# First loads and pooled products of the merge stage moved into the last rows of the attention stage

## The chip, the cores and the metric

The kernel runs on one core of a Trainium2 chip. The metric is the time of one launch on the device, in microseconds, lower is better. Five engines with a queue each share the work: PE (TensorE, matrix products), DVE (VectorE), ACT (ScalarE), POOL (GpSimd) and SP (SyncE, which here only issues DMAs). They wait for each other and for DMAs through semaphores.

## The reference

One layer of a hybrid backbone over 2048 latent tokens and 256 context tokens, width 1024, everything in float32. The normalised input is projected once, and its columns feed four mixers of width 256: a gated MLP over chunks (`gm`), a neighbourhood attention (`na`), a recurrence (`rw`) and centred pooling (`pl`). The end, with which this case deals, is:

```
pl = pool_mix(pl_p) * silu(pl_g)      # (centred mean - p) @ w_grp, times a scale per channel
na = natten_latent(q, k, v, ...) * silu(na_g)   # 32 rows of 64 tokens, 8 x 16 window + 256 context keys

gates = sigmoid(merge_logits)                           # (2048, 4 * 1024)
y = gates[:, 0:1024] * (gm @ w_br[0])
for i in 1..3:
    y = y + gates[:, i*1024:(i+1)*1024] * (branch_i @ w_br[i])   # branches gm, na, rw, pl
out = rmsnorm(x + gate * (y @ w_out), final_g)
```

## The kernel before

Three stages follow each other: `front_stage` (the projections), `recurrence_stage`, and `late_stages`, which calls `attention_stage` (L2053 and on) and `merge_and_output_stage` (L2385). Each stage is a block of five instruction streams, one for each engine, written out by hand; at the end of a block stands a barrier of all engines (it bears the line L2046 in the trace). No scheduler moves anything: the order on an engine is the order of the text, and only semaphores tie the engines.

**Attention.** A loop over 32 rows of the grid runs as a pipeline of depth four: in step n, PE computes the scores of row n, the values of row n-2 (L2353), turns the probabilities of row n-1 (L2335, L2339) and turns the output of row n-2 (L2366). DVE adds the bias and takes the maximum (L2257), copies, divides (L2283) and multiplies by the gate (L2270, one step later). ACT takes the exponentials. Steps 32 to 34 drain the pipeline. Side jobs ride along: POOL computes the pooled differences, DVE scales the eight row blocks of `w_out` by the residual gate (L2294, steps 23 to 30). After the last step come, one after the other, the pooled branch's eight products (PE L2375, four blocks of two) and DVE's scaling and gating of them (L2302, in place in `pg`, which lives in the tile `v_t`). ACT has by then taken SiLU of the pooled gate in one instruction (L2248). SP stores the attention's output in three parts (rows 0-15, 16-27, 28-31; L2144) and the pooled output in four blocks (L2148) to `branchT` in DRAM, waits until all have landed (L2149, L2150), and only then joins the barrier.

**Merge.** The 2048 tokens are handled in four blocks of 512 (n), each in 16 units (branch i = 0..3, pair p = 0..3 of output tiles of 128 columns). Products are made in three passes of split operands: for an operand a, ACT writes `a_hi` (a rounded copy) and DVE `a_lo = a - a_hi` over a's own place; PE adds hi*hi, lo*hi and hi*lo. A unit is 12 matmuls of 512 columns (L2647 to L2649). DVE multiplies each by its gate tile (L2568) and, from the second branch on, adds it to y (L2574). In the first block only, DVE also makes the low parts of the branch weights (L2550, eight halves; `mw`), of the branch rows (L2554; `mb`), of y (L2562) and of `w_out` (L2558). Then y @ w_out follows (tile_upper, tile_lower, tile: L2661 to L2692), the residual and the final norm. At the start SP issues, in this order: the first half of branch 0's weights (L2447), branch 0's rows (L2437), gate tiles 0 and 1 (L2433), the second half (L2451), gate tiles 2 and 3, the whole weights of branch 1 (L2445), branch 1's rows. Weights of branches 2 and 3 are loaded whole, one after pair 1 of each of the first two branches. A unit (0, i, 0) with i > 0 waits for both weight halves of its branch.

Of the kernel before, what the change touches and what calls it, by code (L numbers as in the profile page):

```python
# [2038 lines left out]
def attention_stage(nc, t, s):  # L2039
# [6 lines left out]
    with ExitStack() as ctx:  # L2046
# [24 lines left out]
        pl_ps, pl_out, pl_silu, pl_stored = sem("pool_products"), sem("pool_out_ready"), sem("pool_silu"), sem("pool_stored")  # L2071
# [10 lines left out]
        stored, gate_out, gate_in, scaled = sem("na_stored"), sem("gate_row_out"), sem("gate_rows_in"), sem("wo_scaled")  # L2082
# [21 lines left out]
        def _(sp):  # L2104
# [27 lines left out]
            for first, end in PARTS:  # L2132
                if first == PARTS[1][0]:
# [15 lines left out]
            sp.wait_ge(stored, 64 * len(PARTS))  # L2149
            sp.wait_ge(pl_stored, 16 * NB)  # L2150
# [61 lines left out]
        def _(act):  # L2212
# [35 lines left out]
            A.activation(pg, pg, ACT.Silu).then_inc(pl_silu, 1)  # L2248

        @block.vector  # L2250
        def _(dve):
# [44 lines left out]
            dve.wait_ge(pl_silu, 1)  # L2296
            for b in range(NB):
                dve.wait_ge(pl_ps, b + 1)
# [7 lines left out]
        def _(pe):  # L2306
# [49 lines left out]

            for n in STEPS:
# [10 lines left out]
            pe.wait_ge(diff_set, 2)  # L2368
            pe.wait_ge(plw_in, 16 * 5)
            bvg.after(pe, ROWS - 1, "g")  # L2370
            for b in range(NB):
                if b >= 2:
                    pe.wait_ge(pl_out, b - 1)
                for p in range(2):
                    last = T.matmul(ps[:, 2 * (b % 2) + p, :], plw[:, p, :], dd[:, p, b * BLK:(b + 1) * BLK], start=True, stop=True)  # L2375
                last.then_inc(pl_ps, 1)

def merge_and_output_stage(nc, t, s):
# [8 lines left out]
    with ExitStack() as ctx:  # L2388
# [3 lines left out]
        def split(name, shape):  # L2392
# [4 lines left out]
            return rows, sb(f"{name}_hi", shape, F32R), lo  # L2397
        wo, wo_lo = s["wo_rows"][:, 0:KT * D].rearrange("p (k n) -> p k n", k=KT), s["wo_lo"]
        wo_hi = sb("wo_hi", [P, KT, D], F32R)
        w, w_hi, w_lo = split("mw", [P, 4, 2, D])  # L2400
        y, y_hi, y_lo = split("y", [P, KT, BLK])
        br, b_hi, b_lo = split("mb", [P, 2, 2, BLK])
        gate = sb("m_gate", [P, 4, 2, BLK])
# [3 lines left out]
        w_in, w_h, w_l = [sem(f"w_in{i}") for i in range(5)], sem("w_hi_ready"), sem("w_lo_ready")  # L2407
        b_in, b_h, b_l = [sem("b_in0"), sem("b_in1")], sem("b_hi_ready"), sem("b_lo_ready")
        wo_h, wo_l = sem("wo_hi_ready"), sem("wo_lo_ready")
        gate_in = [[sem(f"gate_in{p}{par}") for par in range(2)] for p in range(NP)]  # L2410
# [12 lines left out]
        w_brs = t["w_br"].rearrange("l i (k p) n -> p (l i) k n", p=P)  # L2423
        plain = lambda a: a.bitcast(F32)
        pair = lambda a, p: a[:, 2 * p:2 * p + 2, :]

        w_part = lambda a, i, h: a[:, 0, :, h * BLK:(h + 1) * BLK] if i == 0 else a[:, i, h, :]

        @block.sync
        def _(sp):  # L2430
            def load_gate(n, i, p):
                src = t["gatesT"][8 * i + 2 * p:8 * i + 2 * p + 2, :, n * BLK:(n + 1) * BLK]
                sp.dma_start(gate[:, p, :, :], src.rearrange("m p t -> p m t")).then_inc(gate_in[p][i % 2], 16)  # L2433

            def load_b(n, i):
                src = t["branchT"][2 * i:2 * i + 2, :, n * BLK:(n + 1) * BLK]
                sp.dma_start(br[:, i % 2, :, :], src.rearrange("m p t -> p m t")).then_inc(b_in[i % 2], 16)  # L2437

# [5 lines left out]
            def load_w(i):  # L2444
                sp.dma_start(w[:, i, :, :], w_brs[:, i, :, :]).then_inc(w_in[i], 16)  # L2445
# [319 lines left out]
```

## Time and profile before

| | us |
|---|---|
| median of 3 runs | 2583.83 (2577.88 to 2587.68) |
| profiled execution | 2572.3 |
| its span, first to last instruction | 2570.6 |
| PE busy | 2270.5 (88%) |
| DVE busy | 1560.4 (61%) |
| ACT busy | 1015.1 (39%) |
| first product of the merge starts at | 2192.36 |
| first product of y @ w_out as a full tile (L2690) | 2271.9 |

### The profile page before, as it was taken

To read this page: it belongs to the slowest core of one execution; us is meant where nothing else is said; L and a number is where in the kernel's file an instruction comes from. 1 tells how busy PE (TensorE), PEld (TensorE's weight loads), DVE (VectorE), ACT (ScalarE), POOL (GpSimd) and SP (SyncE) were. 2 spreads that over 40 slices of the span, in tenths; PEclk is the share of its full clock that TensorE was granted. 3 is DMA by queue.
4 is the path that set the end of the run, shared out by engine and by line. 5 is a ranking of instruction groups with operands and counts; after the bars stand their busy time and mean duration, and the time that the engine had idled before them with its cause. 6 is when DMAs were issued, how large, how long until landed. Compare 5 with 4: busy or idle time off the path is not lost. (4 is left out here: it accounts for less than half of the span.)

```text
span 2570.6 us, 65138 instructions
## 1 busy us (share of the span) xinstructions
PE 2270.5 (88%) x26434; PEld 1854.1 (72%) x26434; DVE 1560.4 (61%) x2583; ACT 1015.1 (39%) x1739; POOL 188.5 (7%) x260
## 2 busy tenths in 40 slices
PE   4999999999899999999668787778695797799998
PEld 2788878888688878888556676667565575677787
DVE  5756656667755456666366666666363577756744
ACT  5454234444522124444345444545323665311111
POOL 0000000000000000000120010000032650000000
PEclk7999999999999999999879999999797899899999
DMA  6343333332333233333321111110356521734542
GB/s 229 110 135 115 108 113 99 112 115 98 119 99 106 88 102 108 110 118 103 92 57 35 34 43 34 35 34 20 115 191 201 134 92 51 278 123 164 197 140 89
DMA packets 253116, 279.50 MB, mean 109 GB/s; under 512 B 34411, under 2 KB 177899, under 8 KB 250347
## 3 DMA queue, kind: packets, MB, share of 16 engines
q1 hardware_dynamic: 250602, 267.94, 32.7%
q10 hardware_dynamic: 2304, 8.39, 0.8%
q8 instruction: 178, 2.92, 0.5%
q14 instruction: 32, 0.25, 0.0%
HBM read 184.66 MB, written 91.62 MB: 107 GB/s over the span
## 5 line engine op out<-in xcount | busy, mean ns | idle before, releaser
L715 PE MATMUL proj_ps<-h_hi,w_hi 128*128 128x512 f32 x1656 | 650.0, 393 | 28.8 <-DVE h_lo L465 20.8
L716 PE MATMUL proj_ps<-h_lo,w_hi 128*128 128x512 f32 x1656 | 646.9, 391 | 0.0
L717 PE MATMUL proj_ps<-h_hi,w_lo 128*128 128x512 f32 x1656 | 646.6, 390 | 0.0
L318 ACT CAST w_hi<-w_raw 128x512 fp32r<-128x512 f32 x420 | 255.1, 621 | 695.8 <-PE proj_ps L717 353.1
L715 PEld LDWEIGHTS proj_ps<-h_hi,w_hi 128*128 128x128 f32 x1656 | 312.5, 189 | 99.1 <-issue 27.7
L717 PEld LDWEIGHTS proj_ps<-h_hi,w_lo 128*128 128x128 f32 x1656 | 312.2, 189 | 65.7
L716 PEld LDWEIGHTS proj_ps<-h_lo,w_hi 128*128 128x128 f32 x1656 | 312.7, 189 | 63.5
L482 DVE TENSOR_TENSOR w_lo<-w_raw,w_hi 128x512 fp32r<-128x512 f32 x420 | 283.1, 688 | 44.2 <-ACT w_hi L318 43.8
L498 DVE TENSOR_TENSOR z_slots<-proj_ps,x_rows 128x512 f32<-128x512 f32 x174 | 120.2, 691 | 171.1 <-PE proj_ps L717 169.0
L498 DVE TENSOR_TENSOR x_rows<-proj_ps,x_rows 128x512 f32<-128x512 f32 x116 | 80.2, 691 | 109.7 <-PE proj_ps L717 103.7
L2647 PE MATMUL late_ps<-mb_hi,mw_hi 128*128 128x512 f32 x256 | 102.5, 400 | 26.3 <-DVE mb_lo L2554 19.3
L1140 DVE TENSOR_TENSOR inv_g<-rw_ps,level_masks 128x512 f32<-128x512 f32 x90 | 62.0, 689 | 95.7 <-PE rw_ps L1308 95.5
L2648 PE MATMUL late_ps<-mb_lo,mw_hi 128*128 128x512 f32 x256 | 101.4, 396 | 0.0
L2649 PE MATMUL late_ps<-mb_hi,mw_lo 128*128 128x512 f32 x256 | 101.3, 396 | 0.0
L1256 ACT COPY inv<-rw_ps 128x512 f32<-128x512 f32 x72 | 42.2, 587 | 148.7 <-PE rw_ps L1308 148.6
L2257 DVE CUSTOM_DVE_ANT_0 scores<-na_ps,bias_windows 128x768 f32<-128x768 f32 x64 | 61.2, 956 | 61.0 <-PE na_ps L2328 40.0
L980 POOL MEMSET rpb_padded<- 60x127 f32 x1 | 0.2, 197 | 1264.2 <-POOLq L89 1264.2
L494 DVE COPY x_rows<-proj_ps 128x512 f32<-128x512 f32 x58 | 40.1, 691 | 73.6 <-PE proj_ps L717 73.6
L2228 ACT ACTIVATE probs<-scores,softmax_stats 128x768 f32<-128x768 f32 x64 | 60.1, 940 | 53.7 <-DVE softmax_stats L2260 53.7
L2690 PE MATMUL late_ps<-wo_hi,y_hi 128*128 128x512 f32 x208 | 81.3, 391 | 0.0
L2691 PE MATMUL late_ps<-wo_lo,y_hi 128*128 128x512 f32 x208 | 80.9, 389 | 0.0
L2692 PE MATMUL late_ps<-wo_hi,y_lo 128*128 128x512 f32 x208 | 80.9, 389 | 0.0
(343 smaller groups left out, 3934.1 us busy)
## 6 DMA issues: line engine op xcount, KB each, us to landing
w_raw<-in_w_in SPq DMA_DIRECT2D x240, 256.0 KB, 3.0
scratch_gatesT<-z_slots SPq DMA_DIRECT2D x128, 256.0 KB, 2.7
m_gate<-scratch_gatesT SPq DMA_DIRECT2D x64, 512.0 KB, 3.9
scratch_zT<-z_slots SPq DMA_DIRECT2D x108, 256.0 KB, 2.4
ada<-in_ada_w SPq DMA_DIRECT2D x4, 2048.0 KB, 15.2
mb_rows<-scratch_branchT SPq DMA_DIRECT2D x16, 512.0 KB, 4.8
x_res<-in_x SPq DMA_DIRECT2D x16, 512.0 KB, 4.6
out<-x_res ACTq DMA_DIRECT2D x16, 512.0 KB, 2.6
```

What stands on the lines that cost most here:

```text
L318: A.copy(wh[:, i, :, :], raw[:, q, :, :]).then_inc(w_hi, 1)
L482: V.tensor_tensor(wl[:, i, :, :], raw[:, W_SOURCE[i], :, :], wh[:, i, :, :].bitcast(F32), ALU.subtract).then_inc(w_lo, 1)
L498: V.tensor_tensor(to, ps[:, BANK[n], :], part[:, {1: 0, 3: 0, 4: 2, 5: 0, 6: 1}[n], :], ALU.add).then_inc(ev, 1)
L715: T.matmul(out, wh[:, i, k, :], hi[:, o, k, :], start=(first and k == 0), stop=False, skip_group_check=not first)
L716: T.matmul(out, wh[:, i, k, :], lo[:, o, k, :], start=False, stop=False, skip_group_check=not first)
L717: last = T.matmul(out, wl[:, i, k, :], hi[:, o, k, :], start=False, stop=(k == 3), skip_group_check=not first)
L2647: T.matmul(o, hi, b_hi[:, i % 2, k, :], start=(k == 0), stop=False)
L2648: T.matmul(o, hi, b_lo[:, i % 2, k, :], start=False, stop=False)
L2649: last = T.matmul(o, lo, b_hi[:, i % 2, k, :], start=False, stop=(k == 1))
L2690: T.matmul(o, y_hi[:, k, rows], wo_hi[:, k, cols], start=(k == 0), stop=False)
L2691: T.matmul(o, y_hi[:, k, rows], wo_lo[:, k, cols], start=False, stop=False)
L2692: last = T.matmul(o, y_lo[:, k, rows], wo_hi[:, k, cols], start=False, stop=(k == KT - 1))
```

## The change

In words: (1) the semaphores and the places of the merge's raw tiles (`merge_gate`, `merge_rows`, `merge_w`) are set up ahead of the attention; they lie over the attention's `q_t`, `k_t` and further on. As soon as the last row's scores are done (q and k are read no more) and `w_out` has been scaled, SP issues branch 0's two weight halves, its rows and its four gate tiles. (2) Pooled blocks 0 and 1 are multiplied by PE inside steps 32 and 33 of the attention, ahead of the turn of the output; blocks 2 and 3 stay behind the last step. ACT's SiLU of the pooled gate is cut into four. (3) SP no longer waits for the landing of the stores ahead of the barrier, but behind it, ahead of the loads of branch 1; DVE waits for the attention's stores before its first multiply. (4) All branch weights are now loaded in column halves, and a unit of pairs 0 or 2 waits only for the half that it reads. (5) In the first block, DVE's low parts stand in another place: weight halves behind pairs 1 and 3 (branch 0) or 0 and 2 (branches 1, 2), the rows' low part behind pair 2 (branch 0) or pair 1; ACT's order follows. The rest only moves tiles.

```diff
@@ attention, SP
             for first, end in PARTS:
...
+                if end == ROWS:
+                    fp.after(sp, ROWS - 1, "S")
+                    sp.wait_ge(scaled, KT)
+                    load_merge_w(sp, t, s, 0, 0)
+                    load_merge_rows(sp, t, s, 0, 0)
+                    load_merge_gate(sp, t, s, 0, 0, 0)
+                    load_merge_gate(sp, t, s, 0, 0, 1)
+                    load_merge_w(sp, t, s, 0, 1)
+                    load_merge_gate(sp, t, s, 0, 0, 2)
+                    load_merge_gate(sp, t, s, 0, 0, 3)
                 bvg.after(sp, end - 1, "g")
...
-            sp.wait_ge(stored, 64 * len(PARTS))
-            sp.wait_ge(pl_stored, 16 * NB)
@@ attention, ACT and DVE
-            A.activation(pg, pg, ACT.Silu).then_inc(pl_silu, 1)
+            for b in range(NB):
+                c = slice(b * BLK, (b + 1) * BLK)
+                A.activation(pg[:, :, c], pg[:, :, c], ACT.Silu).then_inc(pl_silu, 1)
...
-            dve.wait_ge(pl_silu, 1)
             for b in range(NB):
+                dve.wait_ge(pl_silu, b + 1)
@@ attention, PE
+            def pool_products(b):
+                if b == 0:
+                    pe.wait_ge(diff_set, 2)
+                    pe.wait_ge(plw_in, 16 * 5)
+                    fv.after(pe, ROWS - 1, "b1")
+                if b >= 2:
+                    pe.wait_ge(pl_out, b - 1)
+                for p in range(2):
+                    last = T.matmul(ps[:, 2 * (b % 2) + p, :], plw[:, p, :], dd[:, p, b * BLK:(b + 1) * BLK], start=True, stop=True)
+                last.then_inc(pl_ps, 1)
...
                     turn_probs(n - 1)
+                if n >= ROWS and n < ROWS + 2:
+                    pool_products(n - ROWS)
                 if valid(n - 2):
                     bvr.after(pe, n - 2, "o")
...
+            pool_products(2)
+            pool_products(3)
@@ merge, SP
+            sp.wait_ge(s["na_stored"], 64 * 3)
+            sp.wait_ge(s["pl_stored"], 16 * NB)
+            load_merge_w(sp, t, s, 1, 0)
+            load_merge_rows(sp, t, s, 0, 1)
+            load_merge_w(sp, t, s, 1, 1)
...
-                        if n == 0 and i < 2 and p == 1:
-                            load_w(i + 2)
+                        if n == 0 and i < 2 and p in (1, 2):
+                            load_merge_w(sp, t, s, i + 2, p - 1)
@@ merge, ACT (likewise for branches 2 and 3)
             split_w(1, 0)
+            split_b(0, 1)
             split_w(1, 1)
-            split_b(0, 1)
@@ merge, DVE
             split_w(0, 1)
+            dve.wait_ge(s["na_stored"], 64 * 3)
...
-                        if n == 0 and i < 3 and p < 2:
-                            split_w(i + 1, p)
-                        if p == 2 and (i < 3 if n == 0 else i in (1, 2)):
+                        if n == 0 and i < 3 and p in ((0, 2) if i else (1, 3)):
+                            split_w(i + 1, 0 if p < 2 else 1)
+                        if p == (1 if i else 2) and (i < 3 if n == 0 else i in (1, 2)):
                             split_b(n, i + 1)
@@ merge, PE
-                if n == 0 and (i == 0 and p % 2 == 0 or p == 0):
-                    pe.wait_ge(w_l, 2 * i + 2 if i else p // 2 + 1)
+                if n == 0 and p % 2 == 0:
+                    pe.wait_ge(w_l, 2 * i + p // 2 + 1)
@@ new
+def load_merge_w(sp, t, s, i, h):
+    src = t["w_br"].rearrange("l i (k p) n -> p (l i) k n", p=P)[:, i, :, h * BLK:(h + 1) * BLK]
+    sp.dma_start(s["merge_w"][:, i, :, h * BLK:(h + 1) * BLK], src).then_inc(s["w_in"][i][h], 16)
```

How the order changes at three places. The first is the end of PE's attention, before: the values (`v_even`), turned probabilities (`probs`) and outputs (`o_rows`) of rows 30 and 31, then the pooled products (`pool_diff`).

```order
L2353 MATMUL na_ps<-v_even,probs_t 64x64 x24
L2335 MATMUL na_ps<-ident,probs 128x128 x8
L2339 MATMUL na_ps<-ident,probs 128x128 x4
L2366 MATMUL na_ps<-ident,o_rows 128x128
L2353 MATMUL na_ps<-v_even,probs_t 64x64 x24
L2366 MATMUL na_ps<-ident,o_rows 128x128
L2375 MATMUL na_ps<-pool_diff,v_t 128x512 x8
```

The same place on PE in the changed kernel.

```order
L2364 MATMUL na_ps<-v_even,probs_t 64x64 x24
L2346 MATMUL na_ps<-ident,probs 128x128 x8
L2350 MATMUL na_ps<-ident,probs 128x128 x4
L2376 MATMUL na_ps<-pool_diff,v_t 128x512 x2
L2391 MATMUL na_ps<-ident,o_rows 128x128
L2364 MATMUL na_ps<-v_even,probs_t 64x64 x24
L2376 MATMUL na_ps<-pool_diff,v_t 128x512 x2
L2391 MATMUL na_ps<-ident,o_rows 128x128
L2376 MATMUL na_ps<-pool_diff,v_t 128x512 x4
```

Two of the four pooled blocks now stand ahead of the turns of rows 30 and 31. The second place is SP around the end of the attention stage, before: the pooled output's stores, the end of the block, and the merge's first loads.

```order
L2148 DMA scratch_branchT<-v_t 128x2x512 x4
L2046 UNCONDITIONAL_BRANCH
L2429 UNCONDITIONAL_BRANCH
L2447 DMA mw_rows<-in_w_br 128x2x512
L2437 DMA mb_rows<-scratch_branchT 128x2x512
L2433 DMA m_gate<-scratch_gatesT 128x2x512 x2
L2451 DMA mw_rows<-in_w_br 128x2x512
L2433 DMA m_gate<-scratch_gatesT 128x2x512 x2
L2445 DMA mw_rows<-in_w_br 128x2x1024
L2437 DMA mb_rows<-scratch_branchT 128x2x512
```

SP in the changed kernel, from the second row of branch 0's early loads to the loads of branch 1.

```order
L2742 DMA mb_rows<-scratch_branchT 128x2x512
L2737 DMA m_gate<-scratch_gatesT 128x2x512 x2
L2747 DMA mw_rows<-in_w_br 128x2x512
L2737 DMA m_gate<-scratch_gatesT 128x2x512 x2
L2155 DMA scratch_branchT<-na_gate 64x256 x4
L2159 DMA scratch_branchT<-v_t 128x2x512 x4
L2046 UNCONDITIONAL_BRANCH
L2446 UNCONDITIONAL_BRANCH
L2747 DMA mw_rows<-in_w_br 128x2x512
L2742 DMA mb_rows<-scratch_branchT 128x2x512
L2747 DMA mw_rows<-in_w_br 128x2x512
```

Seven loads now stand ahead of the last stores of the attention; behind the block's end only branch 1's three are left. The third place is DVE in branch 0 of the merge, before: low parts of weights (`mw_lo`) and rows (`mb_lo`) between the multiplies (`y_rows<-m_gate,late_ps`).

```order
L2550 TENSOR_TENSOR mw_lo<-mw_rows,mw_hi 128x2x512
L2568 TENSOR_TENSOR y_rows<-m_gate,late_ps 128x1024
L2550 TENSOR_TENSOR mw_lo<-mw_rows,mw_hi 128x1024
L2568 TENSOR_TENSOR y_rows<-m_gate,late_ps 128x1024
L2550 TENSOR_TENSOR mw_lo<-mw_rows,mw_hi 128x1024
L2568 TENSOR_TENSOR y_rows<-m_gate,late_ps 128x1024
L2554 TENSOR_TENSOR mb_lo<-mb_rows,mb_hi 128x1024
L2568 TENSOR_TENSOR y_rows<-m_gate,late_ps 128x1024
```

The same stretch of DVE in the changed kernel.

```order
L2552 TENSOR_TENSOR mw_lo<-mw_rows,mw_hi 128x2x512
L2570 TENSOR_TENSOR y_rows<-m_gate,late_ps 128x1024 x2
L2552 TENSOR_TENSOR mw_lo<-mw_rows,mw_hi 128x2x512
L2570 TENSOR_TENSOR y_rows<-m_gate,late_ps 128x1024
L2556 TENSOR_TENSOR mb_lo<-mb_rows,mb_hi 128x1024
L2570 TENSOR_TENSOR y_rows<-m_gate,late_ps 128x1024
L2552 TENSOR_TENSOR mw_lo<-mw_rows,mw_hi 128x2x512
```

The second weight half of branch 1 now stands behind all four multiplies, and the rows' low part ahead of the last one.

## Rows read from the trace of the kernel before

**Rows 1.** Chain of waits from 2160 to 2195: start us, us, what.
```profile
2184.03 0.37 SPq L2447
...
2184.45 5.44 DMA mb_rows<-scratch_branchT
...
2189.91 1.05 ACT mb_hi L2486
...
2190.99 1.24 DVE mb_lo L2554
...
2192.36 0.76 PE late_ps L2647
2193.13 0.43 PE late_ps L2648
```
**Rows 2.** Timeline, PE and DVE, end of attention: start us, us, engine line, [idle before <-releaser].
```profile
2168.01 0.27 PE L2366 MATMUL na_ps<-ident,o_rows 128*128 128x128 f32 x1
2168.21 0.69 DVE L2287 COPY probs_t<-na_ps 128x512 f32<-128x512 f32 x1 [1.10 <-PE na_ps L2339]
...
2169.24 1.62 PE L2353 MATMUL na_ps<-v_even,probs_t 128*64 128x64 f32 x48 [0.96 <-DVE na_gate L2270]
...
2171.68 0.29 DVE L2270 TENSOR_TENSOR na_gate<-na_ps,na_gate 128x128 f32<-128x128 f32 x1 [0.42 <-PE na_ps L2366]
...
2172.12 7.25 PE L2375 MATMUL na_ps<-pool_diff,v_t 128*128 128x512 f32 x16 [0.48 <-DVE na_gate L2270]
...
2174.21 1.41 DVE L2302 SCALAR_TENSOR_TENSOR v_t<-na_ps,pool_scale,v_t 128x512 f32<-128x512 f32 x2 [2.24 <-PE na_ps L2375]
...
2179.41 1.41 DVE L2302 SCALAR_TENSOR_TENSOR v_t<-na_ps,pool_scale,v_t 128x512 f32<-128x512 f32 x2 [0.31 <-PE na_ps L2375]
2180.85 0.36 SPq L2148 DMA_DIRECT2D scratch_branchT<-v_t  x1
```
**Rows 3.** Timeline, PE alone, starts of branches 1 to 3, first block.
```profile
2207.84 0.47 PE L2647 MATMUL late_ps<-mb_hi,mw_hi 128*128 128x512 f32 x1 [1.56 <-issue]
...
2221.69 0.47 PE L2647 MATMUL late_ps<-mb_hi,mw_hi 128*128 128x512 f32 x1 [2.71 <-issue]
...
2237.14 0.47 PE L2647 MATMUL late_ps<-mb_hi,mw_hi 128*128 128x512 f32 x1 [2.70 <-issue]
```
**Rows 4.** Timeline, DVE alone, the merge's first block.
```profile
2210.93 1.22 DVE L2568 TENSOR_TENSOR m_gate<-m_gate,late_ps 128x1024 f32<-128x1024 f32 x1 [2.06 <-PE late_ps L2649]
2212.18 1.22 DVE L2574 TENSOR_TENSOR y_rows<-y_rows,m_gate 128x1024 f32<-128x1024 f32 x1
2213.33 1.22 DVE L2550 TENSOR_TENSOR mw_lo<-mw_rows,mw_hi 128x1024 fp32r<-128x1024 f32 x1
...
2226.37 1.22 DVE L2568 TENSOR_TENSOR m_gate<-m_gate,late_ps 128x1024 f32<-128x1024 f32 x1 [2.39 <-PE late_ps L2649]
...
2240.23 1.22 DVE L2568 TENSOR_TENSOR m_gate<-m_gate,late_ps 128x1024 f32<-128x1024 f32 x1 [0.80 <-PE late_ps L2649]
...
2254.74 9.16 DVE L2558 TENSOR_TENSOR wo_lo<-wo_rows,wo_hi 128x1024 fp32r<-128x1024 f32 x8
```
**Rows 5.** Chain of waits from 1900 to 2400: the last piece of tile_lower in block 0.
```profile
2264.85 7.25 PE late_ps L2668 x32
```
**Rows 6.** Windows by stage: last column GB/s, ahead of it DMA share and PEclk.
```profile
2208.00:2222.00 14.00, 11.29 (x50) 9.03 (x49) 11.83 (x11) 6.87 (x7) 0.00 (x0) 1.00 0.84 306
2222.00:2237.00 15.00, 12.45 (x48) 9.78 (x46) 12.47 (x12) 3.05 (x3) 0.00 (x0) 0.89 0.67 235
```
**Rows 7.** Windows of 1 us around the clock's fall and rise (PEclk after the busy times).
```profile
2183.00:2184.00 1.00, 0.00 (x0) 0.00 (x0) 0.00 (x0) 0.00 (x0) 0.00 (x0) 1.00 0.10 35
2184.00:2185.00 1.00, 0.00 (x0) 0.00 (x0) 0.00 (x0) 0.00 (x0) 0.00 (x0) 0.78 0.00 0
...
2198.00:2199.00 1.00, 1.00 (x5) 0.82 (x4) 1.00 (x1) 0.00 (x0) 0.00 (x0) 0.89 1.02 397
```
**Rows 8.** SP's own waits from 2150 to 2260.
```profile
SPq L2150 <- DMA scratch_branchT<-v_t: 2.4, 1, 2.4
```
**Rows 9.** Timeline, DVE alone, last two scalings of w_out, one in each attention row.
```profile
2154.10 1.21 DVE L2294 TENSOR_TENSOR wo_rows<-wo_rows,q_t 128x1024 f32<-128x1024 f32 x1
...
2159.38 1.22 DVE L2294 TENSOR_TENSOR wo_rows<-wo_rows,q_t 128x1024 f32<-128x1024 f32 x1
```
**Rows 10.** Issue to landing from 2150 to 2260: count, KB each, median us.
```profile
m_gate<-scratch_gatesT SPq DMA_DIRECT2D x20, 512.0 KB, 4.6
```

More of the change, by code:

```diff
@@ L2366, in _ @@
                     bot.done(T.transpose(ps[:, 7, BR:BR + P], on[:], s["ident"][:]), "OT")
[L2368 to L2376, printed above, removed]
+            pool_products(2)
+            pool_products(3)
 def merge_and_output_stage(nc, t, s):
@@ L2406, in merge_and_output_stage @@
         ps = ctx.enter_context(nc.psum_tensor("late_ps", [P, 4, 2, BLK], F32))
[L2407 to L2408 removed]
+        w_in, w_h, w_l = s["w_in"], sem("w_hi_ready"), sem("w_lo_ready")
+        b_in, b_h, b_l = s["rows_in"], sem("b_hi_ready"), sem("b_lo_ready")
         wo_h, wo_l = sem("wo_hi_ready"), sem("wo_lo_ready")
[L2410 removed]
+        gate_in = s["gate_in"]
         units, gated, added = sem("merge_products"), sem("gated"), sem("y_added")
@@ L2511, in _ @@
             split_w(3, 0)
+            split_b(0, 3)
             split_w(3, 1)
-            split_b(0, 3)
             for n in range(NB):
@@ L2714, in late_stages, with load_merge_gate, load_merge_rows @@
         s["wo_lo"] = ctx.enter_context(nc.sbuf_tensor("wo_lo", [P, KT, D], F32R))
-        with ExitStack() as edges:
-            edges.enter_context(nc.sbuf_tensor("wo_rows_end", [P, 8 * EDGE], F32))
-            s["wo_in"] = ctx.enter_context(nc.semaphore("wo_in"))
-            attention_stage(nc, t, s)
-        merge_and_output_stage(nc, t, s)
+        ctx.enter_context(nc.sbuf_tensor("wo_rows_end", [P, 8 * EDGE], F32))
+        with ExitStack() as under:
+            s["merge_gate"] = under.enter_context(nc.sbuf_tensor("m_gate", [P, 4, 2, BLK], F32))
+            s["merge_rows"] = under.enter_context(nc.sbuf_tensor("mb_rows", [P, 2, 2, BLK], F32))
+            s["merge_w"] = under.enter_context(nc.sbuf_tensor("mw_rows", [P, 4, 2, D], F32))
+        s["wo_in"] = sem("wo_in")
+        s["gate_in"] = [[sem(f"gate_in{p}{par}") for par in range(2)] for p in range(4)]
+        s["rows_in"] = [sem("b_in0"), sem("b_in1")]
+        s["w_in"] = [[sem(f"w_in{i}{h}") for h in range(2)] for i in range(4)]
+        s["na_stored"], s["pl_stored"] = sem("na_stored"), sem("pool_stored")
+        attention_stage(nc, t, s)
+        merge_and_output_stage(nc, t, s)
+def load_merge_gate(sp, t, s, n, i, p):
+    src = t["gatesT"][8 * i + 2 * p:8 * i + 2 * p + 2, :, n * BLK:(n + 1) * BLK]
+    sp.dma_start(s["merge_gate"][:, p, :, :], src.rearrange("m p t -> p m t")).then_inc(s["gate_in"][p][i % 2], 16)
+def load_merge_rows(sp, t, s, n, i):
+    src = t["branchT"][2 * i:2 * i + 2, :, n * BLK:(n + 1) * BLK]
+    sp.dma_start(s["merge_rows"][:, i % 2, :, :], src.rearrange("m p t -> p m t")).then_inc(s["rows_in"][i % 2], 16)
+def load_merge_w(sp, t, s, i, h):
+    src = t["w_br"].rearrange("l i (k p) n -> p (l i) k n", p=P)[:, i, :, h * BLK:(h + 1) * BLK]
+    sp.dma_start(s["merge_w"][:, i, :, h * BLK:(h + 1) * BLK], src).then_inc(s["w_in"][i][h], 16)
 STAGES = (front_stage, recurrence_stage, late_stages)
```

42 lines of the change are left out of this document (13 added, 29 removed).

## The prediction

> **What bounds the kernel now.** I read the page first: PE is busy for 88% of the span and the chain that ended last runs along PE's merge products, so time is won only where PE waits. Then the chain of waits at the hand-over [rows 1]: the merge's first product starts at 2192.36 and hangs, backwards, on DVE's low part of the rows (1.24), ACT's cast (1.05), a DMA of 5.44 and an issue at 2184.03. The timeline shows PE's last attention work, the pooled products, from 2172.12 for 7.25, to 2179.4 [rows 2]. PE thus stands still for 13.0 us, and all of the merge's input travels in that hole. Third, the merge's first block: PE waits again at the starts of branches 1, 2 and 3, 1.56, 2.71 and 2.70 [rows 3]. DVE is the pace there: a multiply starts 1.25 before its add, the next operation 1.15 later [rows 4]. A branch is four multiplies, four adds and three low parts: 4 x (1.25 + 1.14) + 3 x 1.14 = 13.0 us on DVE, against 4 units x 12 matmuls x 0.227 = 10.9 on PE (32 matmuls took 7.25 [rows 5]). The windows show 306 GB/s in such a branch at a DMA share of 0.84 [rows 6], so the DMAs are near full but not over. Last, the clock: it fell to 0.50 in the slice 2184 to 2185, some 5 us after PE stopped, and rose at about 2198.2 [rows 7], 5.8 us after PE began again; meanwhile a matmul took 0.43 instead of 0.227 [rows 1].
>
> **The change, part by part.** The sum is made against the profiled execution (span 2570.6, time 2572.3); the three runs lie higher, median 2583.83, so I carry the difference over to that median.
>
> *End of the attention.* PE's turn of row 31's probabilities ends at 2168.0; the pooled block 0 now comes next, four instructions of 0.43 = 1.7. The turn of row 30's output goes from 2168.01 to 2169.75, its gating ends at 2170.4 (DVE's copy of 2168.21 to 2168.90 is no longer in its way) and the values of row 31 start at 2170.5, not 2169.24 [rows 2]. They take 1.62, block 1 another 1.7, so row 31 is gated at 2174.15 to 2174.45, 2.5 later than the 2171.68 of before. DVE's pooled scaling follows at once: 2174.45, where it was 2174.21. Block 2 may start on PE when block 0 has been read, 2175.9; its result is there 2.05 later (2172.12 to 2174.21 was 2.09 [rows 2]), DVE has it done at 2179.4, block 3 at 2181.1. Before it was 2180.8. The products moved up gain nothing: +0.25. Cutting SiLU in four costs ACT some 0.3 in all and hides, as DVE needs the first quarter only at 2174.45.
>
> *The hand-over.* Before, SP issued its last store at 2180.85 (0.36), waited 2.4 for the landing [rows 8], to 2183.6, and issued the merge's first load at 2184.03; so barrier and branch took 0.4. Now SP arrives at 2181.1 + 0.4 and all engines pass at 2181.95. Branch 0's data are there: SP may issue them when the last scores and the last scaling of w_out are done, 2159.38 + 1.22 = 2160.6 [rows 9]; seven loads of 512 KB are 3.67 MB, 12 us at the 306 GB/s of [rows 6], plus the 4.6 of one load [rows 10]: by 2177 at the latest. Behind the barrier the splits stay on the path, which DMA no longer covers: ACT's cast 1.05, then DVE's two low parts, 1.14 and 1.24, 0.14 to PE: 2181.95 + 1.1 + 1.14 + 1.24 + 0.14 = 2185.5. Before 2192.36: 6.8 earlier.
>
> *Branch 1's loads* are issued when the last pooled store has landed, 2183.9. Three of 512 KB at the 4.6 to landing of [rows 10] and 1.4 more for each next are down by 2191.2. DVE wants the first at 2195.3 (below), so this hides with 4 us to spare.
>
> *Branch 0's products.* PE now stands still for 6 us (2179.65 to 2185.5), longer than the 5 after which the clock fell, so I take it to fall just as PE starts and to come back 5.7 after, at 2191.2, as before. That costs the same 2.8 in both kernels: no gain. Units end at 2190.6, 2193.7, 2196.5, 2199.2. DVE follows: multiplies at 2191.0, 2194.1, low part of the weight half 2195.3, multiply 2196.9, rows 2198.0, multiply 2199.6, second half 2200.7. The rows' low part ends at 2199.2 just as PE is through, so the wait of 1.56 at branch 1 goes.
>
> *Branches 1 to 3.* DVE's first multiply of branch 1 starts at 2202.4, where it was 2210.93 [rows 4]: 8.5 earlier. From here DVE never waits: three stretches of 13.0, to 2241.4, and the last low part of y to 2242.6. Before it lost 2.39, 0.80 and some 0.5 to PE [rows 4] and was through at 2254.74 - the gain has grown to 12.1. On PE the branch 2 wait of 2.71 goes, since its rows' low part stands two operations earlier (done 2209.6, PE needs it at 2210.2); with it goes the half clock that followed, in the slices of 2222 to 2237 at 0.89 [rows 6], 1.6 us of PE. Of the 2.70 at branch 3 1.5 stays, and in the first tile, which waits for y's four low parts, PE waits some 2 more than before. All this is inside DVE's sum.
>
> *Tail of the block.* Last low part of y to the end of tile_lower: before 2254.74 to 2264.85 + 7.25 = 2272.1, 17.4 [rows 4, 5]; now 17.1. So the block ends at 2259.7, 12.4 earlier. Blocks 1 to 3 are untouched and shift whole.
>
> The DMA pieces of 2 KB instead of 4 KB in the weights of branches 1 to 3 I cost at nothing: the gate tiles, of the same 2 KB pieces, make most of those 306 GB/s. If that fails, the second weight halves are late by at most one landing, 4.6, of which 4 is covered. The 3.67 MB that now land in SBUF while rows 28 to 31 are worked: no row shows such a load beside that loop; I bound it from zero to 1.5 us (a tenth of the 14 us it lies beside, at 5.28 a row [rows 9]) and take zero, as multiplies of 128x1024 took the same 1.22 at 306 GB/s [rows 4, 6].
>
> Sum: 0.25 lost, in all 12.4 gained; 2572.3 - 12.4 = 2559.9, and on the median 2583.8 - 12.4 = 2571.4.
>
> **The rivals.**
>
> *The clock stays up.* In the old kernel it fell 5 us into the hole; the new hole is 6. If it falls later or comes back a step earlier, branch 0 runs at 2.4 GHz, up to 2.8 of PE. Worked through DVE's chain the block ends at 2256.9 to 2258: gain 14 to 15, time 2569. Against it: 6 is more than 5.
>
> *A slow start behind the barrier.* In the old trace ACT, DVE and PE had 4.6 us between the barrier's release at 2184.0 and ACT's first cast, which waited for data; anything they did in it was hidden. Now it would show. For it: no row shows these engines starting at once there. Against: SP's first issue came 0.4 after its landing, branch included. Price from 0 to 4.6 at the start; since DVE's chain then wastes less on PE, 8 to 10 of gain is left: time 2574. The Trainium skill, Runtime: NRT & Kernel Launch, section Instruction fetch mechanics, says that a taken branch whose target lies outside the fetched pages stalls until a DMA has brought them. By that rule the change would be in this rival; the trace neither shows nor excludes it.
>
> *The gain is given back inside the merge.* The early part needs loads of branches 1 and 2 closer together. If they land late, the chain is held by DMA at about the old distances and only part of the 6.8 stays: gain 4 to 5, time 2579. Against it: the slack of 4 us above, and 0.84 of DMA share. That the early loads don't become early (SP held behind the stores of part 2) belongs here; those were issued at 2155, so I hold it for unlikely.
>
> *Slower: the clock doesn't come back.* The new first block has waits of about 1.5, 1, 1.7 and 1.7 close together after branch 2. If PE's clock stays at 1.2 GHz through the 16 units, they take 16 x 12 x 0.43 = 82 instead of 46: the block ends at 2290, 18 later than before, time 2601. It decides where more than some 35 us of the block run at half clock (to 2222: about equal). For it: a wait of 2.71 was followed by half clock [rows 3, 6]. Against it: the old kernel, with more waits, lost only one such piece. The Trainium skill, TensorE: Matmul & The Clock Gate, section HAM oscillation, warns that gaps between bursts of products keep throwing the clock back. By it this rival would be likelier than the trace makes it; the granted clock of 0.89 and 1.00 in [rows 6] speaks for a single dip.
>
> **How the numbers follow.** Forecast (10.5 to 14 gained) 0.60; clock stays up 0.15; slow start 0.12; given back 0.09; slower 0.04. Less than 0.5% (12.9 us) either way is about what a measurement of this kernel can't tell from no change, and the forecast's 12.4 lies just at that edge: a good two fifths of its chance and all of the second case fall beyond it, 0.25 + 0.15 plus 0.03 for a slow start on a lucky median. Faster 0.44, within 0.5% 0.50, slower 0.06. The three runs differ by 10 us, so a median of the new kernel moves by some 4 of itself: the range goes from 2562 (clock up, low median) to 2582 (given back, high median).
>
> **What would show it.** Right: branch 0's seven loads issued about 2161; ACT's first cast within 0.2 of 2182; PE's first merge product at 2185.5; the pooled branch done at 2181, not earlier; no wait at branches 1 and 2 and one of 1.5 at branch 3; DVE without a wait from branch 1 on; tile_lower ending near 2260. Wrong: a first cast later than 2183 (slow start), half clock beyond 2195, casts of branch 1's weights that wait past 2195 for their DMA, or attention rows slower than 5.3 us each from 2161 on.

## The result and the profile after

The changed kernel took 2552.27 us (median of 4 runs, 2548.27 to 2556.73) against 2583.5 us (4 runs, 2577.88 to 2587.68): ratio 0.9881, 95% interval 0.9854 to 0.9908. A second comparison on another occasion gave 2552.31 (6 runs) against 2575.17 (21 runs), ratio 0.9927, 0.9906 to 0.9948 (the two medians by themselves divide to 0.9911). The forecast had 2571.4 with a range down to 2562, so both medians lie below it: right in its sign, 12 us gained where the medians differ by 31 and 23, and where the second ratio makes it 19.

The medians scatter by more than a part of this change is worth, so I split two traces of each kernel at three instants: the last start of attention scores, the first merge product, and the last matmul of tile_lower in block 0. Each instant is the start of that matmul. All that the change touches lies behind the first one.

| us | before | before, again | changed | changed, again | forecast for changed |
|---|---|---|---|---|---|
| start to last scores | 2159.9 | 2163.9 | 2164.4 | 2159.6 | as before |
| last scores to first merge product | 32.4 | 32.2 | 25.5 | 25.5 | 25.6 |
| first merge product to end of tile_lower | 79.4 | 79.6 | 72.7 | 73.6 | 73.8 |
| blocks 1 to 3 and the end | 298.9 | 298.9 | 290.7 | 290.7 | 298.9 |
| last scores to end | 410.7 | 410.7 | 388.9 | 389.8 | 398.3 |

The two stages that the forecast worked through agree within 1.1 us. From the last scores to the end the changed kernel is 8.5 to 9.4 us shorter than forecast, and 8.2 of these stand in the fourth row: in blocks 1 to 3, where I had written "untouched". The first median missed the forecast by 19.1; the other 10 or so are in no stage behind the last scores (see the experiment on the scatter).

The chain of waits of the changed kernel at the hand-over (start us, us, what):

```profile
2186.34 1.05 ACT mw_hi L2484
2187.40 0.02 issue
2187.42 1.23 DVE mw_lo L2552
2188.65 1.15 DVE mb_lo L2556
2189.79 0.14 issue
2189.93 0.77 PE late_ps L2650
```

Where [rows 1] had an issue and a DMA of 5.44 ahead of the cast, the chain now begins with the cast itself. The hole on PE (the time that it stands still here) went from 13.0 to 5.9. The timeline around the barrier, all engines but PE's weight loads:

```profile
2165.18 0.39 SPq L2747 DMA_DIRECT2D mw_rows<-in_w_br  x1
...
2178.86 2.72 DVE L2313 SCALAR_TENSOR_TENSOR v_t<-na_ps,pool_scale,v_t 128x512 f32<-128x512 f32 x4
2178.98 2.37 SPq L2155 DMA_DIRECT2D scratch_branchT<-na_gate  x4
2180.32 3.70 PE L2376 MATMUL na_ps<-pool_diff,v_t 128*128 128x512 f32 x8 [1.70 <-DVE v_t L2313]
2181.39 4.53 SPq L2159 DMA_DIRECT2D scratch_branchT<-v_t  x4
...
2184.13 1.41 DVE L2313 SCALAR_TENSOR_TENSOR v_t<-na_ps,pool_scale,v_t 128x512 f32<-128x512 f32 x2 [0.31 <-PE na_ps L2376]
2186.34 1.04 ACT L2484 CAST mw_hi<-mw_rows 128x1024 fp32r<-128x1024 f32 x1 [8.22 <-PEq L2046]
```

SP's last issue ends at 2181.39 + 4.53 = 2185.92 and ACT casts 0.42 later: that is the barrier, branch included. (DVE's last scaling had ended 0.38 ahead of SP's issue.) The pooled scaling ends 21.1 behind the last scores' start; in [rows 2] it was 20.9 (2180.8 - 2159.9).

PE's waits in the first block and the tiles behind it, from the timeline of PE alone, to be compared with [rows 3]:

```profile
2189.93 0.77 PE L2650 MATMUL late_ps<-mb_hi,mw_hi 128*128 128x512 f32 x1 [5.91 <-DVE mb_lo L2556]
2225.73 0.47 PE L2650 MATMUL late_ps<-mb_hi,mw_hi 128*128 128x512 f32 x1 [1.28 <-issue]
2237.56 0.47 PE L2664 MATMUL late_ps<-wo_hi,y_hi 128*128 128x512 f32 x1 [0.66 <-issue]
```

The waits at branches 1 and 2 are gone, 1.28 is left at branch 3. And the lists of PE's waits in blocks 1 to 3 (waited for, us in all, times, longest): of the kernel before, from 2270 to 2580,

```profile
PE late_ps L2647 <- DVE mb_lo L2554: 6.4, 6, 1.1
```

and of the changed kernel, from its tile_lower's end at 2263 to 2553, an empty list. Six waits, at the starts of branches 2 and 3 of blocks 1, 2 and 3. The profile's page of the kernel before had held them too, in the last number of this row, 19.3 where the hand-over accounts for 13.0:

```profile
L2647 PE MATMUL late_ps<-mb_hi,mw_hi 128*128 128x512 f32 x256 | 102.5, 400 | 26.3 <-DVE mb_lo L2554 19.3
```

One of the six on PE of the kernel before, with what DVE did there:

```profile
2316.68 0.50 PE L2647 MATMUL late_ps<-mb_hi,mw_hi 128*128 128x512 f32 x1 [1.06 <-DVE mb_lo L2554]
```

```profile
2313.01 1.22 DVE L2568 TENSOR_TENSOR m_gate<-m_gate,late_ps 128x1024 f32<-128x1024 f32 x1 [0.24 <-PE late_ps L2649]
2314.27 1.23 DVE L2574 TENSOR_TENSOR y_rows<-y_rows,m_gate 128x1024 f32<-128x1024 f32 x1
2315.41 1.22 DVE L2554 TENSOR_TENSOR mb_lo<-mb_rows,mb_hi 128x1024 fp32r<-128x1024 f32 x1
```

DVE makes the rows' low part behind pair 2's multiply and add, which themselves wait for PE's pair 2; it ends at 2316.6, while PE has been through with pair 3 since 2315.6. In the changed kernel the same three stand one pair earlier:

```profile
2301.19 1.22 DVE L2570 TENSOR_TENSOR m_gate<-m_gate,late_ps 128x1024 f32<-128x1024 f32 x1 [0.24 <-PE late_ps L2652]
2302.45 1.22 DVE L2576 TENSOR_TENSOR y_rows<-y_rows,m_gate 128x1024 f32<-128x1024 f32 x1
2303.59 1.22 DVE L2556 TENSOR_TENSOR mb_lo<-mb_rows,mb_hi 128x1024 fp32r<-128x1024 f32 x1
```

### The profile page after: what moved, and what is told of

Its sections match the earlier page's. It is cut to its first block and busy times, and to the rows that moved or that the text cites. A ratio compares the mean times of both kernels' runs of the same rounds, so it can differ in the third digit from the quotient of the medians.

```text
span 2553.3 us, 65150 instructions
## 1 busy us (share of the span) xinstructions
PE 2260.6 (89%) x26434; PEld 1847.5 (72%) x26434; DVE 1559.2 (61%) x2583; ACT 1015.4 (40%) x1742; POOL 188.6 (7%) x260
## 5 line engine op out<-in xcount | busy, mean ns | idle before, releaser
L494 DVE COPY x_rows<-proj_ps 128x512 f32<-128x512 f32 x58 | 40.0, 690 | 73.6 <-PE proj_ps L717 73.5
```

## Experiments

The kernels whose median is not given below ran once each: 2566.35 us with branch 0's loads behind the barrier, 2561.82 with the stores' landing awaited ahead of it, 2558.47 with the pooled products last, 2562.08 with the first block's old order (the kernel before: 2574.52 once, beside them), and 2550.82 with PE kept busy. One run can't tell them apart, so they are read by the stages of their traces.

**The move of the rows' low part, alone, both ways.** First the changed kernel without it in blocks 1 to 3:

```diff
-                        if p == (1 if i else 2) and (i < 3 if n == 0 else i in (1, 2)):
+                        if p == (1 if i and n == 0 else 2) and (i < 3 if n == 0 else i in (1, 2)):
                             split_b(n, i + 1)
```

> The changed kernel, but in blocks 1 to 3 DVE makes the branch rows' low part behind pair 2 again, not behind pair 1 (the first block stays as changed). Theory A (this move, which the prediction overlooked, stops a wait of 1.06 us at six branch starts, about 1.3 us each with the pipeline's refill): slower than the changed kernel by 7 to 9 us, waits of 1.06 for mb_lo back at six places, and from the last attention scores' start to the end about 397 instead of 388.9. Theory B (the extra gain of blocks 1 to 3 comes from the weights' and gates' loads or from the clock, not from this order): within 2 us of the changed kernel.

Measured: 2560.91 us (6 runs), ratio to before 0.9946 (0.9931 to 0.9960), 8.6 us above the changed kernel in the same comparison. Its trace has 397.1 from last scores to end, the stages ahead of block 1 as in the changed kernel (25.5 and 72.7), blocks 1 to 3 at 298.9, and this list of PE's waits there:

```profile
PE late_ps L2650 <- DVE mb_lo L2556: 6.4, 6, 1.1
```

Then the kernel before with that one edit:

```diff
-                        if p == 2 and (i < 3 if n == 0 else i in (1, 2)):
+                        if p == (1 if n else 2) and (i < 3 if n == 0 else i in (1, 2)):
```

> The kernel before with this one edit: in blocks 1 to 3 the rows' low part stands behind pair 1. Theory A: 7 to 9 us faster than before (ratio 0.9965 to 0.9973), the six waits gone, last scores to end about 402.5 instead of 410.7. Theory B: no change, ratio 1.000 within its interval.

Measured: 2567.73 us (10 runs), ratio 0.9967 (0.9951 to 0.9982); last scores to end 402.6, blocks 1 to 3 at 290.8, no wait there. Theory A holds in both directions, to 0.1 us in the traces; theory B falls. The move is worth 8.1 to 8.2 us by the pairs of traces, some 1.36 for each wait shown as 1.06. This trace has the loads of before and its blocks 1 to 3 take the same 290.8 as those of the changed kernel (290.7), so nothing there hangs on the weights' loads in halves.

**How large is the change, and where is the scatter.** Both kernels again, unedited.

> The changed kernel again, unedited, for a second trace and a tighter ratio. Theory A (all of the gain lies behind the last scores, 21.8 us by the two traces; the 31 us between the medians holds some 10 us of scatter): ratio nearer to 0.9915 (22 us), last scores to end 388 to 390. Theory C (the change also makes the stages ahead of the hand-over shorter, by code placement or the like): ratio stays at 0.988 and the last scores start some 10 us earlier than in the kernel before.

> The kernel before again, unedited. Shows the scatter of a ratio where nothing changed, and a second start of the last scores. Theory A: last scores to end 410 to 411 as in the first trace, while their start (2159.7 there) moves by up to 10 us. Theory C: their start lies near 2170 in most runs, against 2160 for the changed kernel.

Measured: the changed kernel 0.9927 (0.9906 to 0.9948); before against itself 0.9999 (0.9985 to 1.0014). The start of the last scores was 2159.6 (changed) and 2163.9 (before), against 2164.4 and 2159.9 in the first pair. Over all 14 traces of this study it lies between 2157.4 and 2169.1, with no tie to the kernel, since the stages ahead of it are the same in all; behind it the two traces of before agree to 0.1 us, those of the changed kernel to 0.9. Theory C falls. The gain behind the last scores is 21 to 22; the 31 us between the first medians lie outside what the stages show, and where in the runs without a trace the other 9 were was not shown.

**Branch 0's loads, behind the barrier instead of beside the attention.** The seven load calls follow the lines taken out, and stand ahead of the last line.

```diff
-                if end == ROWS:
-                    fp.after(sp, ROWS - 1, "S")
-                    sp.wait_ge(scaled, KT)
...
@@ merge, SP
...
             sp.wait_ge(s["na_stored"], 64 * 3)
```

> The changed kernel, but branch 0's seven loads are issued at the start of the merge stage, behind the barrier, not beside the last attention rows. Read by stages. Theory A (the hidden loads carry the hand-over): from the last scores to the first merge product 30 us instead of 25.5, as the first cast waits 4.6 us for its DMA; branch 1's loads queue behind them, so that first product to the end of tile_lower grows from 72.7 to some 76. Theory B (moving the stores' waits behind the barrier does it and loads of that size would land in time anyway): 25.5 to 27.

Measured: last scores to first merge product 31.8, to the end of tile_lower 73.0 more. ACT in that trace:

```profile
2196.80 1.04 ACT L2480 CAST mw_hi<-mw_rows 128x1024 fp32r<-128x1024 f32 x1 [13.99 <-DMA mw_rows<-in_w_br]
2198.47 1.04 ACT L2484 CAST mb_hi<-mb_rows 128x1024 fp32r<-128x1024 f32 x1 [0.62 <-DMA mb_rows<-scratch_branchT]
```

The first load was issued at 2191.02 and the cast came 5.8 later. Theory A's place is right, its price too low by 1.8: the first cast waited 5.8 and not 4.6, and DVE waits for the second load as well; what made the first load slower than 4.6 was not separated. So the early issue carries 6.3 of the 6.9 us of the hand-over. The expected queueing of branch 1's loads, 3 us, didn't come: 73.0 is 0.3 above 72.7, and the clock, which came back later here, explains that (below).

**The stores' landing, awaited ahead of the barrier.**

```diff
                 sp.dma_start(t["branchT"][6:8, :, c].rearrange("m p t -> p m t"), pg[:, :, c]).then_inc(pl_stored, 16)
+            sp.wait_ge(stored, 64 * len(PARTS))
+            sp.wait_ge(pl_stored, 16 * NB)
```

> The changed kernel, but SP waits for all stores to land ahead of the barrier, as before. Theory A: the barrier is 2.3 us later, last scores to first merge product 27.8 instead of 25.5, first product to wo_lo about 1 to 2 shorter or equal, since branch 1's loads start at the same instant. Theory B (barrier is held by something else): 25.5.

Measured: 28.2, then 73.1: theory A holds for the barrier, and the part expected to be equal or shorter is 0.4 longer, again by the clock (below). SP's own wait in that trace:

```profile
SPq L2161 <- DMA scratch_branchT<-v_t: 2.6, 1, 2.6
```

The same wait stands in the changed kernel too (2.6), only behind the barrier, where no engine but SP pays for it. The two terms overlap: 6.3 and 2.7 together are more than 6.9, since without early loads the casts wait for DMA in any case.

**The pooled products, all behind the last step.**

```diff
-                if n >= ROWS and n < ROWS + 2:
-                    pool_products(n - ROWS)
...
-            pool_products(2)
-            pool_products(3)
+            for b in range(NB):
+                pool_products(b)
```

> The changed kernel, but all four pooled blocks are multiplied behind the last attention step, as before. Theory A (the two early blocks delay the attention by what they save): last scores to first merge product 25.2 to 25.7 instead of 25.5, last pooled scaling within 0.3 of the changed kernel's 25.0 behind the scores' last start. Theory B (they do their work in PE's idle time and save it at the end): 27 to 29.

Measured: 24.7, then 72.8. Theory B falls, and 24.7 lies below the 25.2 to 25.7 of theory A as well: the early products do not just gain nothing, they cost 0.8 (the last pooled scaling ends 20.3 behind the last scores, not 21.1). Row 31's values wait for row 30's gating, and that for the pooled block put ahead of it. In the trace with them last, PE takes them in one piece, as it did in [rows 2], and DVE's scalings follow from 1.5 behind the gating:

```profile
2178.52 7.19 PE L2376 MATMUL na_ps<-pool_diff,v_t 128*128 128x512 f32 x16
```

```profile
2178.72 0.29 DVE L2281 TENSOR_TENSOR na_gate<-na_ps,na_gate 128x128 f32<-128x128 f32 x1 [0.42 <-PE na_ps L2389]
2180.55 1.41 DVE L2313 SCALAR_TENSOR_TENSOR v_t<-na_ps,pool_scale,v_t 128x512 f32<-128x512 f32 x2 [1.53 <-PE na_ps L2376]
```

**The first block's order of before** (DVE, ACT and PE's waits; loads as changed). ACT's lines are left out here.

```diff
-                        if n == 0 and i < 3 and p in ((0, 2) if i else (1, 3)):
-                            split_w(i + 1, 0 if p < 2 else 1)
-                        if p == (1 if i else 2) and (i < 3 if n == 0 else i in (1, 2)):
+                        if n == 0 and i < 3 and p < 2:
+                            split_w(i + 1, p)
+                        if p == (1 if n else 2) and (i < 3 if n == 0 else i in (1, 2)):
@@ PE
-                if n == 0 and p % 2 == 0:
-                    pe.wait_ge(w_l, 2 * i + p // 2 + 1)
+                if n == 0 and (i == 0 and p % 2 == 0 or p == 0):
+                    pe.wait_ge(w_l, 2 * i + 2 if i else p // 2 + 1)
```

> The changed kernel with the first block's order of before: DVE makes both weight halves of the next branch behind pairs 0 and 1 and the rows' low part behind pair 2, ACT likewise, and PE waits for both halves at a branch's start; loads and blocks 1 to 3 as changed. Theory A (the order matters once DVE is the pace): waits of 2 to 3 us back at the starts of branches 2 and 3, first product to end of tile_lower 75.5 to 77 instead of 72.7. Theory B (DVE's sum of work sets the end, whatever its order): 72.7 to 73.6.

Measured: 25.5, then 76.0, with the old waits at branches 2 and 3 back on PE:

```profile
2220.84 0.47 PE L2650 MATMUL late_ps<-mb_hi,mw_hi 128*128 128x512 f32 x1 [2.72 <-issue]
...
2234.72 0.47 PE L2650 MATMUL late_ps<-mb_hi,mw_hi 128*128 128x512 f32 x1 [2.72 <-issue]
```

Theory A: against 72.7 and 73.6 the order is worth 2.4 to 3.3 us in the first block, though DVE's sum of work is the same; with the old order PE waits for DVE at a branch's start and DVE then waits for PE's first unit (0.82 at branches 2 and 3). Part of the 3.3 is the clock, which came back later here (below).

The kernel before took 79.4 for this stage, 3.4 more. It had a wait of 1.56 at branch 1 as well, which this trace doesn't have, and a second stretch of half clock: 0.89 over the 15 us of [rows 6] is 3.3 us at 1.2 GHz, half of which, 1.7, is lost. The two add up to the 3.4; that is an estimate, as no run separates them.

**Is the clock worth anything in the hand-over.** Two products nobody reads behind the last pooled block, three behind the barrier:

```diff
             pool_products(3)
+            for _ in range(2):
+                T.matmul(ps[:, 7, :], plw[:, 0, :], dd[:, 0, 0:BLK], start=True, stop=True)
@@ merge, PE
+            for _ in range(3):
+                T.matmul(ps[:, 3, 1, :], s["ident"][:], s["wo_rows"][:, 0:BLK], start=True, stop=True)
```

> The changed kernel with five fp32 products whose results nobody reads: two behind the last pooled block (into a free bank), three behind the barrier ahead of the first merge product. They fill PE's hole of 5.9 us and take nothing from other engines. Theory A (the hole makes PE's clock fall, and that costs branch 0 some 1.5 to 2.8 us, of which DVE's chain passes on 1 to 2.4): granted clock 1.00 throughout, first product still 25.5 behind the last scores, first product to end of tile_lower 70.3 to 71.7 instead of 72.7. Theory B (DVE's work sets the end, the clock costs nothing): 72.7.

Measured: 25.5, then 71.1 (0.75 of the hole on PE was left ahead of the first merge product). In the changed kernel, windows around the hand-over (PEclk third from the end) showed

```profile
2185.00:2186.00 1.00, 0.00 (x0) 0.00 (x0) 0.54 (x1) 0.00 (x0) 0.00 (x0) 1.00 1.04 393
2186.00:2187.00 1.00, 0.00 (x0) 0.00 (x0) 0.00 (x0) 0.66 (x1) 0.00 (x0) 0.65 1.03 375
...
2193.00:2194.00 1.00, 1.00 (x5) 0.80 (x4) 0.00 (x0) 0.81 (x1) 0.00 (x0) 0.93 1.01 383
```

in its second trace

```profile
2183.00:2184.00 1.00, 0.00 (x0) 0.00 (x0) 1.00 (x2) 1.00 (x2) 0.00 (x0) 0.71 0.31 102
2190.00:2191.00 1.00, 1.00 (x5) 0.86 (x4) 0.37 (x1) 0.85 (x1) 0.00 (x0) 0.88 0.18 53
```

and here

```profile
2183.00:2193.00 10.00, 9.25 (x37) 6.52 (x36) 6.05 (x6) 4.32 (x5) 0.00 (x0) 1.00 0.70 243
```

A window that the clock changes in tells when: 0.65 between 1.00 and 0.50 is a fall at 2186.3. PE began again at 2189.9 and had full clock at 2193.1, so it worked at 1.2 GHz for 3.2 us; in the second trace the fall came at 2183.4, the restart at 2185.1 and the rise at 2190.2, which is 5.1. Half of each is lost: 1.6 and 2.55. Taken from 72.7 and 73.6 that leaves 71.1 and 71.0, and 71.1 is what was measured with the clock held. The same subtraction brings four more traces there: 72.7, 73.0, 72.8 and 73.1 (rows behind pair 2, loads behind the barrier, pooled products last, waits ahead of the barrier), with rises 3.1, 3.7, 3.4 and 4.0 behind the restart, all come to 71.1. Theory A holds, and the 0.9 between the two traces of the changed kernel is explained. In the kernel with the first block's old order the rise came 5.6 behind the restart, a loss of 2.8; without it its 76.0 is 73.2, so the order by itself is worth about 2.1.

Blocks 1 to 3 took 292.1 in this trace, 1.4 more than elsewhere; it has two waits for y's low part in the last block (0.31 and 0.51) that no other trace has. There is one trace of this kernel, and their cause stays open. In all, last scores to end was 388.8, no shorter than the 388.9 of the changed kernel's first trace: the gain in the first block was lost again behind it.

**New versions.** The experiments point to what makes up the 25.5 and the 72.7: the splits behind the barrier, the early pooled products, the clock. Version 1 makes branch 0's casts behind SiLU on ACT, and two of its low parts between the pooled scalings on DVE, with the split tiles set up ahead of the attention like the raw ones:

```diff
+            act.wait_ge(s["w_in"][0][0], 16)
+            A.copy(s["w_hi"][:, 0, :, 0:BLK], s["merge_w"][:, 0, :, 0:BLK]).then_inc(s["w_h"], 1)
...
                 last.then_inc(pl_out, 1)
+                if b == 1:
+                    dve.wait_ge(s["w_h"], 1)
+                    V.tensor_tensor(s["w_lo"][:, 0, :, 0:BLK], s["merge_w"][:, 0, :, 0:BLK], s["w_hi"][:, 0, :, 0:BLK].bitcast(F32), ALU.subtract).then_inc(s["w_l"], 1)
...
```

> New version 1: the changed kernel, and branch 0's hi parts (ACT, behind SiLU) and two of its three low parts (DVE, between the pooled scalings) are made ahead of the barrier. Theory A (behind the barrier only these splits keep PE waiting): pooled scaling ends 1.3 us later, but the first merge product starts 0.4 behind the barrier, 23 instead of 25.5 after the last scores; DVE's chain is ahead by as much: last scores to end 386 to 387 instead of 389; 2 to 3 us faster than the changed kernel, ratio to before 0.991. Theory B (DVE just does the same work earlier and the pooled part pays for it): 388 to 389.

Version 2 is version 1 with the pooled products last; version 3 adds the two unread products behind them.

> New version 2: version 1 with the pooled products all behind the last step, which saved 0.9 by itself. Theory A (both gains add): first merge product 22 to 22.5 after the last scores, last scores to end 385 to 386. Theory B (the pooled blocks' results come later than DVE's free slots, so the low parts no longer fit): 386.5 to 388. Either way the fastest of all so far if A, ratio to before about 0.990.

> New version 3: version 2 with two products that nobody reads behind the last pooled block. The hole on PE is short by then (about 3 us), so the clock falls in some runs only. Theory A: granted clock 1.00 in the hand-over, first product to end of tile_lower up to 2 us shorter than in version 2 if the clock fell there, equal if not. Theory B (two more products keep PE's part of the barrier open): first merge product 0.5 to 1.5 later than in version 2.

| | runs | median us | ratio to before (95%) | scores to first product | to end of tile_lower | scores to end |
|---|---|---|---|---|---|---|
| changed, again | 6 | 2552.31 | 0.9927 (0.9906 to 0.9948) | 25.5 | 73.6 | 389.8 |
| version 1 | 4 | 2547.56 | 0.9900 (0.9876 to 0.9924) | 23.0 | 73.9 | 387.6 |
| version 2 | 6 | 2546.88 | 0.9904 (0.9883 to 0.9926) | 22.6 | 71.2 | 384.5 |
| version 3 | 6 | 2543.21 | 0.9885 (0.9866 to 0.9904) | 22.6 | 71.2 | 384.5 |

The first line is from another comparison than the versions (before: 2575.17 there, 2570.43 here), so its median can't be set against theirs; the stages can. Version 1's first product came as expected, but its scores to end stayed 0.6 above the range. Its clock fell all the same and was back 5.7 behind the restart, and without the price of that, 2.85, its 73.9 is 71.0 again:

```profile
2179.92 3.70 PE L2388 MATMUL na_ps<-pool_diff,v_t 128*128 128x512 f32 x8 [1.70 <-DVE v_t L2319]
2187.06 0.76 PE L2658 MATMUL late_ps<-mb_hi,mw_hi 128*128 128x512 f32 x1 [3.44 <-PEq L2046]
```

In version 2 the hole on PE is 3.8 and the clock did not fall, so that it ends at 384.5, 0.5 below the range of theory A, which had only added the two gains:

```profile
2180.97 1.40 DVE L2319 SCALAR_TENSOR_TENSOR v_t<-na_ps,pool_scale,v_t 128x512 f32<-128x512 f32 x2
2183.21 1.23 DVE L2560 TENSOR_TENSOR mw_lo<-mw_rows,mw_hi 128x1024 fp32r<-128x1024 f32 x1 [0.83 <-PEq L2046]
2183.36 0.47 PE L2656 MATMUL late_ps<-mb_hi,mw_hi 128*128 128x512 f32 x1 [3.82 <-PEq L2046]
```

PE starts with the barrier now. Its hole is longer than version 1's 3.44, but no other of 1.70 stands ahead of it: the pooled products are one piece of 7.19 again. Version 3's unread products had no fall to prevent; its trace is as long as version 2's behind the scores, and its lower median is within the scatter of what comes ahead (its scores started at 2157.4, the earliest of all). Versions 2 and 3 end 4.4 to 5.3 us earlier behind the scores than the changed kernel.

## Why the prediction was wrong, step by step

- *"Blocks 1 to 3 are untouched and shift whole."* This step failed, and it is 8.2 of the 8.5 to 9.4 us that the stages came out shorter than forecast. The condition in the diff reads `p == (1 if i else 2)` for every block and `i in (1, 2)` for blocks 1 to 3, so the low part moved there as well. The text on the change (its point 5) says "in the first block", which is wrong for this line; so is the description of the kernel before, which has DVE make the low parts of the rows and of y "in the first block only" (the rows' line L2554 runs 16 times, in all four blocks). The trace of before had the row: PE waits 6.4 us in six pieces for `mb_lo` behind 2270. I read PE's waits up to 2272 alone, and passed over the 19.3 of the profile's page. The old wait of 1.06 seemed small where the profile's page puts PE at 9 tenths nearly throughout. What the runs showed in the step's place: the move ends six waits, and taken back alone it costs 8.2 us, put alone into the kernel before it gains 8.1, a third of a per cent.
- *End of the attention, +0.25.* Right in size: it measured 0.2 (21.1 against 20.9). Undoing it gave 0.8 back, more than it cost, since the old kernel's products had also waited for row 31's gating, which the change no longer asks for.
- *Hand-over, 6.8.* Right, by the mechanism forecast: 6.9, and 6.7 by the second traces. The seven loads were issued between 2165.2 and 2169.5, the last one 16 us ahead of the barrier. The rest of the attention was not slower for them: the pooled scaling ends 21.1 behind the last scores with them, and just so in the trace that has them behind the barrier.
- *Slow start behind the barrier.* Refuted: ACT's first cast came 0.42 after SP's last issue. The Trainium skill, Runtime: NRT & Kernel Launch, section Instruction fetch mechanics, warns of a stall at a taken branch to a page not fetched; no such stall shows here, as the 0.42 holds the branch and the barrier. Whether the branch's target lay within the fetched pages no trace shows.
- *The clock.* I had it fall some 5 us after PE's stop and come back 5.7 after its restart, as in the trace of before, at an equal price of 2.8. It fell 2.3 after the stop (2186.3 against 2184.0) and came back 3.2 and, in the second trace, 5.1 after the restart. In the second trace it fell 4.2 after the stop. The price was 1.6 and 2.55: this is why the stage took 72.7 and 73.6 and not 73.8. Reading a delay of 5 us from one trace was the mistake, even though its effect was small.
- *Given back inside the merge.* Didn't happen: DVE's chain from branch 1's first multiply, at 2205.52, to the last low part of y, at 2245.7, took 40.2, without a wait; forecast 40.2.
- *Clock stays down, slower.* Didn't happen: the granted clock was 1.00 from 2193.1 to 2551.5. (The 16 units at full clock take 43.6 by the forecast's own 0.227, not the 46 written there.) What spoke for this rival was a half clock that followed the wait of 2.71 at branch 2, and the forecast also saw 1.6 us of PE go with that wait. The runs don't bear that link out: the kernel with the old order waits 2.72 twice with the clock at 1.00, and in the trace of the kernel before with the one edit the second stretch of half clock came at 2211.9, behind branch 1. What brings it stays open.
- *The order in the first block.* Forecast as the end of the 2.71 wait and a part of 2.70, inside DVE's sum; alone it is worth about 2.1.
- *The weights in halves.* Their pieces of 2 KB instead of 4 were priced at nothing. Nothing in the stages is left over for them, but no run changed them alone.
- *The median.* I took the difference of two traces over to the median; the first gain was larger than the traces bear out, the second ratio agrees with them within its interval (13 to 24 us, against 21 to 22 in the traces).

## What to carry to other kernels

Where an edit sits in a loop over blocks, evaluate its condition for every block before calling any of them untouched, and ask the trace for the bounding engine's waits to the very end, however busy that engine looks. A wait of 1 us that recurs can be worth more than a hand-over: moving one DVE instruction two places up gave 8.2 us, the whole hand-over 6.9, of it 6.3 by the early loads. Work moved ahead of a barrier pays when it fills idle slots, and costs when it stands ahead of what the next step waits for, as the pooled products did.

## What I had not expected of the hardware

- A wait that the profile shows as 1.06 us cost 1.36 us of time (8.2 over six). At 2316.68 in the kernel before, the product ahead is counted as busy for 0.39 where its stream goes on every 0.23 (0.16 of the price), and the product behind the wait had 0.34 to its successor instead of 0.23 (0.11 more).
- The clock's fall and rise keep no fixed distance to PE's stop and restart. Over the eleven traces with a fall it came 2.2 to 5.2 us after PE's last product, and the rise 3.1 to 6.0 after its first; the loss is half of the latter. A longer hole did not always bring the fall where a shorter one did: 3.44 with one of 1.70 shortly ahead brought it, 3.82 behind 7.19 of unbroken work did not. Each of these is one trace, and whether the work ahead of the hole or chance decided was not shown.
- 3.67 MB landing in SBUF left the instructions of the attention rows at the same durations: the values of a row took 1.62, the exponentials 0.94 to 0.95, as in the kernel before. The window of the changed kernel in which they landed:

```profile
2163.00:2178.00 15.00, 12.92 (x198) 9.40 (x197) 7.09 (x19) 10.57 (x16) 0.00 (x0) 1.00 0.88 272
```
